# Probabilities and values of the attention as high and low parts: three fp32r products in place of one fp32 product

## What is computed

```python
s = jnp.einsum('bqghd,bgqkd->bghqk', qc, kg).astype(jnp.float32) + bias
p = masked_softmax(s, (dist >= 0)[:, :, None])
return jnp.einsum('bghqk,bgqkd->bqghd', p.astype(vg.dtype), vg)      # o_s
...
p_w = masked_softmax(s_w, mask_w[:, None, None])
o_w = jnp.einsum('bjghqk,bjkgd->bjqghd', p_w.astype(vwb.dtype), vwb).reshape(Bsz, S, G, HPG, DH)
o = (gates[:, :, 0, :, :, None] * o_c + gates[:, :, 1, :, :, None] * o_s
     + gates[:, :, 2, :, :, None] * o_w)
return o.reshape(Bsz, S, N_HEADS * DH) @ w_out
```

## Time and profile before

| | |
|---|---|
| median of 3 runs | 2104.81 us (2104.70 to 2104.82) |
| the profiled execution, its own time | 2104.84 us |
| its span | 2103.1 us |
| granted TensorE clock over the span | 0.999 |
| PE busy | 2094.3 us, 100% of the span |
| DVE, ACT, POOL busy | 1268.8, 1010.7, 77.1 us |
| stretch with the attention of the 16 heads | about 193 to 346 us of the span |

### The profile page before, as it was taken

One profiled execution on the slowest core, in us unless ns is written; L12 is line 12 of the kernel. 1 busy time (PEld: TensorE's weight loads), 2 busy tenths in 40 slices (PEclk: granted clock), 3 DMA queues, 4 the chain that ended last, 5 costly groups with the idle time before them and its releaser, 6 DMA issues.

```text
span 2103.1 us, 29342 instructions
## 1 busy us (share of the span) xinstructions
PE 2094.3 (100%) x10132; PEld 1765.1 (84%) x10132; DVE 1268.8 (60%) x1715; ACT 1010.7 (48%) x1342; POOL 77.1 (4%) x141
## 2 busy tenths in 40 slices
PE   9999999999999999999999999999999999999998
PEld 8888888888888888888888888888888888888887
DVE  7767666555555555545556866857757655455464
ACT  6465665544444444444444555444454454444444
POOL 1001221000000000000000000000000000000000
PEclk9999999999999999999999999999999999999999
DMA  8576444656566556656665555555555556556564
GB/s 299 189 269 232 143 131 162 209 196 204 199 209 199 199 199 199 209 192 201 200 202 192 188 183 186 187 177 179 190 176 183 176 184 206 192 199 201 190 241 148
DMA packets 112823, 411.28 MB, mean 196 GB/s; under 512 B 12802, under 2 KB 12842, under 8 KB 112352
## 3 DMA queue, kind: packets, MB, share of 16 engines
q1 hardware_dynamic: 106848, 386.97, 55.5%
q0 software_dynamic: 5744, 23.07, 3.2%
q10 hardware_dynamic: 144, 0.03, 0.0%
HBM read 394.01 MB, written 2.14 MB: 188 GB/s over the span
## 4 chain that ended last, share of the span: by engine, by line
PE 99%; DMA 0%; ACT 0%; DVE 0%; DVEq 0%; SPq 0%; issue 0%
PE set L1655 24%; PE set L1657 24%; PE set L1656 24%; PE set L1681 13%; PE set L1689 7%; PE misc L1929 1%; PE misc L1808 1%; PE set L1779 1%; PE misc L1881 1%; PE misc L1868 1%; PE misc L2057 0%; PE set L1783 0%; PE misc L1854 0%; PE set L1739 0%; PE misc L1882 0%; PE misc L2026 0%
## 5 line engine op out<-in xcount | busy, mean ns | idle before, releaser
L948 DVE TENSOR_TENSOR w_hl<-raw,w_hl 128x1024 fp32r<-128x1024 f32 x729 | 891.9, 1225 | 737.4 <-ACT w_hl L579 735.4
L579 ACT ACTIVATE w_hl<-raw 128x1024 fp32r<-128x1024 f32 x729 | 770.9, 1059 | 960.9 <-PE set L1657 776.8
L1655 PE MATMUL set<-w_hl,x_hl 128*128 128x512 f32 x1408 | 553.3, 393 | 0.0
L1657 PE MATMUL set<-w_hl,x_hl 128*128 128x512 f32 x1408 | 548.5, 390 | 0.0
L1656 PE MATMUL set<-w_hl,x_hl 128*128 128x512 f32 x1408 | 547.8, 389 | 0.0
L1657 PEld LDWEIGHTS set<-w_hl,x_hl 128*128 128x128 f32 x1408 | 264.3, 188 | 55.7
L1656 PEld LDWEIGHTS set<-w_hl,x_hl 128*128 128x128 f32 x1408 | 264.4, 188 | 54.4
L1655 PEld LDWEIGHTS set<-w_hl,x_hl 128*128 128x128 f32 x1408 | 264.3, 188 | 54.1
L1681 PE MATMUL set<-x_hl,w_hl 128*128 128x512 f32 x1216 | 295.4, 392 | 0.0
L1681 PEld LDWEIGHTS set<-x_hl,w_hl 128*128 128x128 f32 x1216 | 222.3, 188 | 42.7 <-DVE t L969 0.2
L1689 PE MATMUL set<-x_hl,w_hl 128*128 128x256 f32 x1216 | 163.0, 284 | 0.0
(11 more groups left out here) (332 smaller groups left out, 1732.4 us busy)
## 6 DMA issues: line engine op xcount, KB each, us to landing
raw<-in_weights SPq DMA_DIRECT2D x730, 512.0 KB, 3.4
turn<-f_b POOLq DMA_DIRECT2D x11, 512.0 KB, 3.2
bias_g<-bias POOLq DMA_DIRECT2D x4, 572.0 KB, 3.4
h<-in_x SPq DMA_DIRECT2D x4, 512.0 KB, 7.1
bias<-u_dram POOLq DMA_DIRECT2D x1, 2048.0 KB, 13.8
h<-in_x_rows POOLq DMA_DIRECT2D x1, 2048.0 KB, 11.3
turn<-h POOLq DMA_DIRECT2D x4, 512.0 KB, 3.5
m_turn<-m_t POOLq DMA_DIRECT2D x4, 512.0 KB, 3.1
```

The costliest lines, as they stand in the source:

```text
L579: a(high, whole, ACT.Copy).then_inc(hi_ready, 1)
L948: tt(low, whole, high.bitcast(F32), ALU.subtract).then_inc(lo_ready, 1)
L1655: mm(o, hl[:, kt, 0, x], w[:, 0, c], start=first and k == 0, stop=False, skip_group_check=True)
L1657: last = mm(o, hl[:, kt, 1, x], w[:, 0, c], start=False, stop=True, skip_group_check=True)
```

## The change

`prob_t` and `v_g` become float32r, that is, their rounded high parts. Two new tiles hold the low parts: `prob_lo` (written by DVE in a new step `low_probs`, two subtractions of 128x384, one operand in PSUM) and `v_lo` (written by POOL, two subtractions of 128x256 per group, each behind its copy). `values` then does three float32r products in place of each full float32 one, in the same PSUM bank. PE's `values` and the next `transposes` wait for `ptl_ready`, which DVE signals, in place of `pt_ready`, which ACT signals. POOL's loop over groups 1 and 2 is written out. The new tiles share memory with tiles that are dead by then.

```diff
-        v_g = sb("v_g", [P, 2, TT, DH], scope=s1)
+        v_g = sb("v_g", [P, 2, TT, DH], F32R, scope=s1)
...
+        with ExitStack() as heads_only:
+            prob_lo = sb("prob_lo", [P, 2, TRI], F32R, scope=heads_only)
+            v_lo = sb("v_lo", [P, 2, TT, DH], F32R, scope=heads_only)
...
-            prob_t = sb("prob_t", [P, 2, TRI], scope=s1c)
+            prob_t = sb("prob_t", [P, 2, TRI], F32R, scope=s1c)
...
                     for b in range(2):
-                        g.tensor_copy(v_g[:, b, :, :], v_sw[:, b, :, bass.ds(gi * DH, DH)])
+                        v_b = v_sw[:, b, :, bass.ds(gi * DH, DH)]
+                        own.link(g.tensor_copy(v_g[:, b, :, :], v_b))
+                        g.tensor_tensor(v_lo[:, b, :, :], v_b, v_g[:, b, :, :].bitcast(F32), ALU.subtract)
...
-        with pool.Fori(1, GROUPS - 1) as gi:
+        for gi in range(1, GROUPS - 1):
             group(gi)
...
+        def low_probs(gi, n):
+
+            dve.wait_ge(pt_ready, gi * HPG + (n + 1))
+            if real(gi, n - 1):
+                dve.wait_ge(o_done, gi * HPG + n)
+            for b in range(2):
+                last = tt(prob_lo[:, b, :], m[2 + b][:, 0:TRI], prob_t[:, b, :].bitcast(F32), ALU.subtract)
+            last.then_inc(ptl_ready, 1)
+
+        def head_step(gi, slot):
+            n = slot // 2
+            if slot % 2 == 0:
+                if real(gi, n - 3):
+                    take_head(gi, n - 3)
+                if real(gi, n - 2) and not last_head(gi, n - 2):
+                    low_probs(gi, n - 2)
+            elif last_head(gi, n - 2):
+                low_probs(gi, n - 2)
...
             if real(gi, n - 1):
-                pe.wait_ge(pt_ready, gi * HPG + n)
+                pe.wait_ge(ptl_ready, gi * HPG + n)
...
-            pe.wait_ge(pt_ready, gi * HPG + (n + 1))
+            pe.wait_ge(ptl_ready, gi * HPG + (n + 1))
...
             for b in range(2):
-                mm(m[1][:, 0:S], v_g[:, b, 0, :], prob_t[:, b, 0:S], start=b == 0, stop=False)
-                mm(m[1][:, P:S], v_g[:, b, 1, :], prob_t[:, b, S:TRI], start=False, stop=False)
+                for t, keys_of in ((0, slice(0, S)), (1, slice(S, TRI))):
+                    o = m[1][:, t * P:S]
+                    mm(o, v_g[:, b, t, :], prob_t[:, b, keys_of], start=b == 0 and t == 0, stop=False)
+                    mm(o, v_g[:, b, t, :], prob_lo[:, b, keys_of], start=False, stop=False)
+                    mm(o, v_lo[:, b, t, :], prob_t[:, b, keys_of], start=False, stop=False)
```

More of the change, by code:

```diff
@@ L192, in program @@
         gate = sb("gate", [P, HEADS, 3, TT], scope=s1)
-        g_sig = sb("g_sig", [3 * HEADS, S], scope=s1)
         q_t = sb("q_t", [P, HPG, S], scope=s1)
-        v_g = sb("v_g", [P, 2, TT, DH], scope=s1)
+        v_g = sb("v_g", [P, 2, TT, DH], F32R, scope=s1)
         v_c = sb("v_c", [STACK, GROUPS, DH], F32R, scope=s1)
         v_cg = sb("v_cg", [STACK, DH], F32R, scope=s1)
+        valid = sb("valid", [P, TT], scope=s1)
+        with ExitStack() as heads_only:
+            prob_lo = sb("prob_lo", [P, 2, TRI], F32R, scope=heads_only)
+            v_lo = sb("v_lo", [P, 2, TT, DH], F32R, scope=heads_only)
+        g_sig = sb("g_sig", [3 * HEADS, S], scope=s1)
         w2 = sb("w2", [P, 2, 2, DH], scope=s1)
         pos = sb("pos", [P, 2, CB], scope=s1)
-        valid = sb("valid", [P, TT], scope=s1)
         rel = sb("rel", [BUCKETS + 1, HEADS], scope=s1)
@@ L322, in program @@
     pt_done, pt_ready, o_done, o_ready = sem("pt_done"), sem("pt_ready"), sem("o_done"), sem("o_ready")
+    ptl_ready = sem("ptl_ready")
     up_sig, ft_done, fh_ready, f_ready = sem("up_sig"), sem("ft_done"), sem("fh_ready"), sem("f_ready")
@@ L1226, in take_head @@
             tt(low, src, high.bitcast(F32), ALU.subtract).then_inc(o_ready, 1)
+        def low_probs(gi, n):
[14 more added lines that the diff above has]
+                low_probs(gi, n - 2)
         def heads_out(gi, slots=NB):
-            return {2 * n: lambda n=n: take_head(gi, n - 3) for n in range((slots + 1) // 2) if real(gi, n - 3)}
+            return {slot: lambda slot=slot: head_step(gi, slot) for slot in range(slots)}
         def softmax_step(gi, n):
```

## The result

| | before | after |
|---|---|---|
| median of 17 runs each | 2104.81 us (2104.63 to 2105.26) | 2108.32 us (2108.09 to 2110.04) |
| ratio, 95% interval | | 1.0019 (1.0012 to 1.0025) |
| span of the profiled execution | 2103.1 us | 2106.6 us |
| granted TensorE clock over the span | 0.999 | 0.999 |

The change costs 3.5 us, 0.17%. The forecast was 2107.4, +2.6 us; the time lies in the range of 2103.2 to 2109.0 and within 0.2% of before. What was missed is 0.9 us of waiting, on a path that the prediction had priced at "Nothing". So the interest lies in the parts of the 3.5 us, each of which can be read in the trace; most were then measured by themselves. Of 28 runs of after (11 of them made beside the last experiment), 19 took 2108.1 to 2108.7 us and 9 took 2109.8 to 2110.4, and since both traces of it are of the lower kind, what the upper kind is stays open.

The account below looks back on a forecast made before the run. The prediction took PE to bound the kernel. It added +1.1 (products), +1.1 (first head) and +0.4 (last head), +2.6 us on the profiled 2104.84, for 2107.4 us, with a range of 2103.2 to 2109.0.

Parts of the forecast that it names:

- What bounds the kernel: Whole kernel: PE's stream bounds it, 99% of the chain; only its length and new PE waits count.
- The products, +1.1: PE's `values`: wide products gain 0.07 each, narrow ones lose 0.11 through weight loads; +1.1 us over 16 heads.
- rival 1: PE's narrow products go as fast as the fp32r transposes (0.079) or faster: 2104.4, down to 2103.3 us; chance 17%.
- Rival 3: PE's fp32r products below 256 columns lose their rate; at 0.22 us per narrow product 2118.0 us; chance 9%.
- The first head, +1.1: Group 0, slot 5: `low_probs` waits for ACT and delays the maxima, `masked` and PE; +1.1 us (0.9 to 1.4).
- POOL ... Nothing: POOL's two subtractions per group end in its 3.37 us idle gap before the values that use them; no cost.
- The pair: DVE's two `low_probs` subtractions per head: 0.48 us each, 0.96 together, between 0.7 and 1.2.
- Steady heads hidden: Ordinary heads: DVE's wait for ACT's exponentials, at least 1.34 us, covers the two subtractions, so `masked` does not move.
- Rival 4: DVE's two subtractions outlast their cover in steady heads, from 1.64 us; at 2.0 us the time is 2110.3; chance 5%.
- The last head, +0.4: Last head's `values`: 0.67 us of room after ACT's copy against 0.96 of DVE subtractions; +0.4 us (0 to 0.6).
- Rival 2: The PE waits at the first and last head are hidden, leaving the products alone: 2105.9 us; chance 8%.

Follow-up runs that it names:

- the last experiment: The changed kernel with the moves of experiments six to eight, but only the 256-column products split and the 128-column ones kept full fp32: 2102.78 us.
- The second and third experiment: The kernel of the first experiment with its narrow products streaming 64 columns instead of 128: 2105.70 us; or having 64 weight columns instead of 128: 2102.70 us.
- The first experiment: The kernel before with each full fp32 product made three fp32r products of the high parts, without low parts or new waits: 2105.84 us.
- the sixth experiment: The changed kernel, complete, with POOL's copies and subtractions of group 0's values moved ahead of the first head: 2107.77 us.
- experiments six to eight: The changed kernel with group 0's POOL values earlier (2107.77 us), then also the first head's subtractions later (2107.08), then also the last head's subtractions started separately (2106.98).

## Why the prediction was right or wrong

**What bounds the kernel: right.** The time outside the 16 heads moved by no more than 0.1 us, and the granted clock stayed at 0.999.

**The products, +1.1: right, 1.2 measured.** The step that decided the sign, 0.110 for a narrow product from its weight load, holds for the second and third of each three: with half the columns the time moved by 0.14 us, with half the weight columns by 3.1. The first of each three takes 0.061 and the wide product behind it 0.05 more, so the sum of 0.33 came out as costed, though it isn't three times 0.110. The row that the 0.110 was taken from, line 2033, is a full float32 product; that an fp32r load costs the same was an assumption there, and it held. With this falls rival 1: three narrow products, with what the next wide one takes longer, cost 0.33 and not 0.24. Rival 3, a lost rate below 256 columns, falls too: with a lighter load the same 128 columns come every 0.058, close to the 0.066 that the prediction had as the price of the columns alone. Why the fp32r transposes come every 0.079, with load records of 140 ns where those of 64 weight columns last 134, no run here shows.

The page "TensorE: Matmul & The Clock Gate" of the Trainium skill, section "LDWEIGHTS (loading the stationary operand)", lets the load time go by the columns of weights alone. The second and third experiment agree in kind. An estimate by that rule gives 53 ns for 64 columns; the spacing fell to 0.058, which is also what the 128 streamed columns take, so these runs can't test the 53.

**The first head, +1.1: the step failed on "POOL ... Nothing".** The pair itself was right: 0.93 for a forecast of 0.96, `masked` is what PE waits for, and without `v_lo` the first head costs 1.13 beside the products, as forecast. But the prediction asked of POOL's two subtractions only whether they end in POOL's gap. They do (the second `v_lo` of group 1 ends at 242.14 + 0.74 = 242.88, and the load for `values` starts at 246.84), though they and the copies take 3.5 us from 239.39 and not 2.7. It didn't ask what DVE does meanwhile. Measured by removal, `v_lo` costs 1.05 us (0.84 against its own before), though no engine waits for it. In the traces 0.6 of that is at the first head, where DVE is the path, and 2 x 0.2 at slot 4 of groups 1 and 2. DVE's records there are 0.77 longer (3.12 against 2.35), but about 0.16 of it takes the place of a wait that the 1.1 had in it, for ACT's copy: 0.77 later, DVE finds the copy done. The term should have been 1.7, and one of 0.4 for groups 1 and 2 was missing. Rows of before had a hint that I passed by: instructions of 30 columns on DVE, beside POOL's copies, and line 1213 again 7 us later, with POOL idle.

```profile
200.90 0.74 POOL L487 COPY v_g<-v_sw 128x256 f32<-128x256 f32 x2
201.26 0.42 DVE L1213 TENSOR_TENSOR prob_hl<-prob,share 128x30 fp32r<-128x30 f32 x1
...
208.08 0.18 DVE L1213 TENSOR_TENSOR prob_hl<-prob,share 128x30 fp32r<-128x30 f32 x1
```

**Steady heads hidden: right for what was priced, with one cover too few.** The room ahead of `make_share` took the pair everywhere. By form, against the earlier trace rows:

```profile
L1240 DVE TENSOR_TENSOR prob_lo<-misc,prob_t 128x384 fp32r<-128x384 f32 x32 | 16.3, 551 | 4.6 <-ACT prob_t L702 4.5
L1202 DVE RECIPROCAL total<-total 128x6 f32<-128x6 f32 x16 | 3.1, 192 | 17.4 <-ACT prob L688 17.4
```

The instruction takes 551 ns (estimated 555). The idle time ahead of line 1202 fell from 35.2 to 17.4, and not to 21, since 4.5 us of it now stand ahead of line 1240, as a wait for ACT. Rival 4, a pair longer than its cover, falls: in the tight place of the earlier trace rows line 1202 still has 0.24 us of idle time ahead of it, at 243.87. But `masked` is not all that DVE owes PE in an even slot. `take_head` comes before the pair and signals `o_ready`; I didn't give it a slack of its own, and it had none in slot 4.

**The last head, +0.4: right in place and releaser, a little less in size.** 0.48 is idle ahead of the load, about 0.3 of it ahead of the products.

**Rival 2, the waits are hidden: wrong.** The first experiment is just that case, and after lies 2.3 to 2.5 us above it.

**The sum by what was measured.** Products 1.2, first head 0.93 + 0.77, `scores` 0.4, last head 0.3: 3.6 us, against 3.5. Against the forecast of 2.6 that is +0.1 for the products, +0.77 and +0.4 for the POOL step, -0.17 for the wait for ACT and the pair's size at the first head, -0.1 for the last head.

## What to carry to other kernels

Before a full fp32 product is split into three fp32r products, ask whether the columns cover the weight load that each of them brings: here 256 columns gained 0.07 us a product and 128 lost 0.11, so the best version split the wide ones alone (2102.78 against 2104.81 and 2108.32). Work added to an idle engine is not free because its own queue has room: look up what the others do at that moment (here DVE beside POOL), and whether one of them is on the path. Moving such work only helps if nothing of the kind stands at its new place, as the sixth experiment showed. And for every signal of an engine that a new step stands near, give a slack of its own; an early reorder helps only up to the next input or the next entry of the queue, as experiments six to eight showed.

## What was not expected of the hardware

DVE, with two operands in SBUF, and POOL slowed each other. DVE's pair of 128x1024 subtractions took 3.12 us instead of 2.35 beside POOL's `v_lo`, a 128x512 instruction 0.99 instead of 0.75; POOL's 128x256 subtraction took 1.59 beside that pair and 0.74 in group 1. Both DVE numbers came back when only the POOL work was removed. Instructions of DVE with one operand in PSUM kept their time: line 975 took 0.68 and line 1232 took 0.42 in group 1 of after, both with a `v_lo` running beside them, as lines 969 and 1226 did before. A cost of this kind shows in no wait: it is only a longer record on an engine whose work did not change.

The Trainium skill has the rule on its page "SBUF — State Buffer", section "🔬 SBUF: two separate sides": VectorE with two SBUF inputs and GpSimd use a pair of ports under an exclusive lock, when the GpSimd instruction reads SBUF, and the one that comes second waits. The traces agree in kind: the 0.77 that the pair lost is about the length of one `v_lo` (0.74 to 0.77). In size they don't always: in group 1 `v_lo` still had 0.45 us to run when line 1034 began (240.52 + 0.74 against 240.81), and that line grew by 0.24 only.

The second is the size of the load's part: halving a product's weight columns took the spacing of the second and third narrow product from 0.110 to 0.058 us, and halving the streamed columns changed the whole time by 0.14 us only.
